# Attention by pairs of heads, and expert tokens of four experts transposed together

## The reference

```python
def block_attention(q, k, v):        # 8 query heads of 64, 2 key heads; blocks of 128 queries
    s = jnp.einsum('bqkgd,bskd->bkgqs', qblk, k) * scale
    p = jax.nn.softmax(s, axis=-1)
    return jnp.einsum('bkgqs,bskd->bqkgd', p, v)

def expert_choice_ffn(h, router_w, w_gu, w_down):   # 16 experts, each picks cap = 2 * n / 16 tokens
    aff = jax.nn.softmax(xf @ router_w, axis=-1)
    gate, idx = lax.top_k(aff.T, cap)
    xin = xf[idx]
    a, u = jnp.split(jnp.einsum('ecd,edf->ecf', xin, w_gu), 2, axis=-1)
    out = jnp.einsum('ecf,efd->ecd', jax.nn.silu(a) * u, w_down) * gate[..., None]
    return jnp.zeros_like(xf).at[idx.reshape(-1)].add(out.reshape(-1, D))
```

## Time and profile before

| | before |
|---|---|
| median of the runs | 4650.71 us (4649.28 to 4650.81, 3 runs) |
| profiled execution | 4647.39 us |
| its span, first to last instruction | 4645.6 us |
| granted TensorE clock, mean | 0.945 of 2.4 GHz |
| attention stage | 427 us, once |
| experts stage | 914 and 912 us |

### The profile page before, as it was taken

How to read it: one execution, slowest core, us unless ns; L and a number is a source line. 1 busy time by engine, 2 the same in 40 slices (tenths; PEclk the granted TensorE clock), 3 DMA queues, 4 the chain that set the end, 5 groups by cost and what they waited for, 6 DMA issues and landing times. The chain is left out here.

```text
span 4645.6 us, 59698 instructions
## 1 busy us (share of the span) xinstructions
PE 4148.2 (89%) x23973; PEld 3289.7 (71%) x23973; DVE 1825.1 (39%) x3112; ACT 1245.0 (27%) x2593; POOL 200.7 (4%) x304
## 2 busy tenths in 40 slices
PE   5798999999759999999699999999768299999996
PEld 1454456665339999998588888888644199999995
DVE  4324355552351111111248888888832611111111
ACT  1211135552201111111244454444423011111111
POOL 0000000000000000001000000000000001000000
PEclk8899989999879999999799999999889599999998
DMA  6201100003487888777410101110032478888884
GB/s 224 86 14 58 35 1 1 1 1 118 174 273 244 252 249 248 239 239 239 123 29 26 31 16 31 31 31 17 7 137 95 129 224 252 251 252 251 251 249 160
DMA packets 522238, 614.81 MB, mean 132 GB/s; under 512 B 16460, under 2 KB 466632, under 8 KB 521449
## 3 DMA queue, kind: packets, MB, share of 16 engines
q1 hardware_dynamic: 502216, 543.33, 36.0%
q0 software_dynamic: 16832, 58.73, 5.0%
q10 hardware_dynamic: 3040, 10.68, 0.6%
HBM read 558.86 MB, written 53.84 MB: 132 GB/s over the span
## 5 line engine op out<-in xcount | busy, mean ns | idle before, releaser
L1385 PEld LDWEIGHTS moe_pgu<-moe_xT,mw_w 128*128 128x128 f32 x8192 | 1118.7, 191 | 15.6 <-issue 15.6
L1385 PE MATMUL moe_pgu<-moe_xT,mw_w 128*128 128x160 f32 x8192 | 1126.4, 300 | 3.0 <-ACT moe_xT L1431 3.0
L1461 DVE TENSOR_TENSOR moe_hT<-moe_sg,moe_pgu 128x160 f32<-128x160 f32 x256 | 82.3, 322 | 1028.0 <-PE moe_pgu L1385 944.9
L1398 PE MATMUL moe_pol<-mw_w,moe_hT 128*128 128x256 f32 x2048 | 474.6, 385 | 0.8 <-DVE moe_hT L1461 0.8
L1642 PE MATMUL rec_pz<-step_hnT,rec_w 128*128 128x256 f32 x1920 | 425.1, 380 | 10.8 <-DMA rec_w<-in_r_w_in 8.8
L1398 PEld LDWEIGHTS moe_pol<-mw_w,moe_hT 128*128 128x128 f32 x2048 | 379.0, 190 | 52.8 <-DVE moe_hT L1461 1.3
L1642 PEld LDWEIGHTS rec_pz<-step_hnT,rec_w 128*128 128x128 f32 x1920 | 362.8, 191 | 59.7 <-DMA rec_w<-in_r_w_in 9.1
L1439 ACT ACTIVATE moe_sg<-moe_pgu 128x160 f32<-128x160 f32 x256 | 77.8, 304 | 1124.9 <-PE moe_pgu L1385 1124.9
L1431 ACT ACTIVATE moe_xT<-moe_pxt,step_modcol 128x128 f32<-128x128 f32 (+1 forms) x512 | 172.5, 417 | 534.2 <-PE moe_pxt L1371 534.2
L1646 PE MATMUL rec_pz<-rec_w,step_hnT 128*128 128x256 f32 x1280 | 284.8, 381 | 15.2 <-ACT rec_zg L1717 15.2
L1646 PEld LDWEIGHTS rec_pz<-rec_w,step_hnT 128*128 128x128 f32 x1280 | 241.5, 191 | 49.8 <-ACT rec_zg L1717 18.0
(11 more groups left out here) (316 smaller groups left out, 4648.7 us busy)
## 6 DMA issues: line engine op xcount, KB each, us to landing
mw_w<-in_moe_w_gu SPq DMA_DIRECT2D x256, 1024.0 KB, 10.1
mw_w<-in_moe_w_down SPq DMA_DIRECT2D x128, 1024.0 KB, 10.2
mod_w_ring<-in_mod_w SPq DMA_DIRECT2D x24, 1024.0 KB, 14.4
mw_w<-in_mod_w SPq DMA_DIRECT2D x24, 1024.0 KB, 14.3
rec_w<-in_r_w_in SPq DMA_DIRECT2D x40, 512.0 KB, 3.9
scratch_xm<-op_x ACTq DMA_DIRECT2D x20, 512.0 KB, 2.6
scratch_xn<-op_xn POOLq DMA_DIRECT2D x20, 512.0 KB, 5.1
hin_w<-in_e_w_in SPq DMA_DIRECT2D x12, 512.0 KB, 6.7
```

Source lines behind the costliest of these rows:

```text
L1385: m = nc.tensor.matmul(pgu[2 * (f % 2) + part][:, :], w[:, j, k, (f % 2) * P:(f % 2 + 1) * P], xT[:, k, :], start=(k == 0), stop=(k == KD ...
L1398: m = nc.tensor.matmul(pol[q // 2][:, (q % 2) * SW:(q % 2 + 1) * SW], hT[:, k, 0:CL], w[:, 8 + q, k, :], start=(k == 0), stop=(k == KD - 1))
```

## The change

Attention: the items become 40 pairs of heads, the eight context pairs first, then the 32 latent ones. Scores of both heads are issued chunk by chunk, one head in the upper and one in the lower 64 rows of the array, into two buffers of three banks. The transposes of both heads are cut in groups of four (five groups for a latent pair) through one PSUM bank; ScalarE copies the first three groups, VectorE the fourth and fifth. The value products of the pair before stand in four pieces between the groups, both heads in turn, in two halves of the array's columns. ScalarE does one exponential per head over all columns, after its copies; VectorE takes maxima over 1,024 and 256 columns.

Experts: the loops are written out. Context tokens are gathered for four experts at once (128 rows, by a new index list `idx_four` that the route makes with four small matmuls), transposed as whole 128x128 tiles and put into a ring of eight experts' tokens in `hnT`; latent tokens are gathered and transposed per expert. GpSimd's copies of indices go, and its gathers no longer wait for the scatter to land.

```diff
-    items = [(2 * pr + r, t, 0 if t < CT else CT, CT if t < CT else KT - CT)
-             for pr in range(4) for t in range(NT) for r in range(2)]
+    pairs = [(pr, t, 0, CT) for pr in range(4) for t in range(CT)] + [(pr, t, CT, KT - CT) for pr in range(4) for t in range(CT, NT)]
+    tiles = [[(r, a) for r in range(2) for a in range(nk)] for _, _, _, nk in pairs]
+    groups = [[tl[g:g + 4] for g in range(0, len(tl), 4)] for tl in tiles]
+    by_dve = [g >= 3 for gr in groups for g in range(len(gr))]
-        s_ps = ps("s_ps", [P, 3 * 512])
-        t_ps = [ps(f"t_ps{i}", [P, 512]) for i in range(4)]
+        s_ps = ps("s_ps", [P, 2, 3 * 512])
+        t_ps = ps("t_ps", [P, 512])
...
@@ TensorE @@
+            def scores(i, j):
+                pr, t, k0, nk = pairs[i]
+                k, n = chunks[i][j]
+                for r in range(2):
+                    if i:
+                        pe.wait_ge(exped, 2 * (i - 1) + r + 1)
+                    nc.tensor.matmul(s_ps[:, r, k * P:(k + n) * P], qT[64 * r:64 * r + HD, pr, t * P:(t + 1) * P],
+                                     kT[64 * r:64 * r + HD, pr // 2, (k0 + k) * P:(k0 + k + n) * P],
+                                     start=True, stop=True).then_inc(qk, 1)
+            def transposes(i, g):
+                group = groups[i][g]
+                pe.wait_ge(normed, 2 * i + 1 + max(r for r, _ in group))
+                copied(pe, gfirst[i] + g)
+                for n, (r, a) in enumerate(group):
+                    m = nc.tensor.transpose(t_ps[:, n * P:(n + 1) * P], p[:, i % 2, r, a * P:(a + 1) * P], S["ident"][:, :])
+                m.then_inc(tr, 1)
             for i in range(N):
+                ng = len(groups[i])
+                for g in range(ng):
+                    transposes(i, g)
+                    if g == 0 and i + 1 < N:
+                        for j in range(len(chunks[i + 1])):
+                            scores(i + 1, j)
+                    if i and (g or ng == 1):
+                        nk = pairs[i - 1][3]
+                        cuts = [nk * x // max(1, ng - 1) for x in range(ng)] if ng > 1 else [0, nk]
+                        a0, a1 = cuts[max(0, g - 1)], cuts[max(1, g)]
+                        if a1 > a0:
+                            products(i - 1, a0, a1)
...
@@ VectorE @@
             for i in range(N):
                 if i + 1 < N:
-                    softmax(i + 1)
-                if i >= 1:
+                    maxes(i + 1)
+                copy(i, 3)
+                if i + 1 < N:
+                    normalise(i + 1, 0)
+                copy(i, 4)
+                if i + 1 < N:
+                    normalise(i + 1, 1)
+                if i:
                     output(i - 1)
...
...
@@ experts @@
+        ring = hnT[:, :, :].rearrange("p k (s c) -> p k s c", c=CC)
+        turns = [("c", 0), ("l", 0)]
+        for e in range(1, NE):
+            turns += [("l", e)] + ([("c", e // 4)] if e % 4 == 0 else [])
+        def coming(e):
+            return [t for t in (("l", e + 1), ("c", (e + 1) // 4)) if t in turns and (t[0] == "l" or (e + 1) % 4 == 0)]
+            def transposes(turn, g):
+                src = xl if kind == "l" else xc
+                for j in range(4):
+                    m = nc.tensor.transpose(pxt[:, j * P:(j + 1) * P], src[:, (4 * g + j) * P:(4 * g + j + 1) * P], S["ident"][:, :])
+                m.then_inc(tr, 1)
-            with pe.Fori(0, NE - 1) as e:
-                expert(e, False)
-            expert(NE - 1, True)
+            for e in range(NE):
...
+                moves = [(turn, g) for turn in coming(e) for g in range(2)]
+                if moves:
+                    transposes(*moves[0])
+                pe.wait_ge(multiplied, NF * (e + 1))
                 for q in range(4):
...
+                    if q + 1 < len(moves):
+                        transposes(*moves[q + 1])
...
@@ GpSimd @@
+            for e in range(NE):
+                if e + 1 < NE:
+                    gather_l(e + 1)
+                if e % 4 == 0 and e + 4 < NE:
+                    gather_c(e // 4 + 1)
                 scatter(e)
...
@@ route @@
+            for j in range(4):
+                m = nc.tensor.matmul(pt[32 * j:32 * j + CAP[0], 4 * NE:], topf[:, 0, 0:CAP[0]], S["ident"][0:NE, j:NE:4],
+                                     start=True, stop=True, tile_position=(0, 32 * j))
```

More of the change, by code:

```diff
@@ new lines, in transposes, with products @@
+            def transposes(i, g):
[5 more added lines that the diff above has]
+                m.then_inc(tr, 1)
+            def products(i, a0, a1):
+                pr, t, k0, nk = pairs[i]
+                if a0 == 0:
+                    copied(pe, gfirst[i + 1])
+                    if i:
+                        pe.wait_ge(o_out, i)
+                for a in range(a0, a1):
+                    for r in range(2):
+                        m = nc.tensor.matmul(o_ps[64 * r:64 * r + HD, 0:P], v[:, k0 + a, (pr // 2) * HD:(pr // 2 + 1) * HD],
+                                             pT[:, i % 2, r * nk + a, :], start=(a == 0), stop=(a == nk - 1))
+                if a1 == nk:
+                    m.then_inc(pv, 1)
@@ new lines, in _ @@
+            for j in range(len(chunks[0])):
+                scores(0, j)
+            for i in range(N):
+                ng = len(groups[i])
[10 more added lines that the diff above has]
+                            products(i - 1, a0, a1)
@@ L964, in _ @@
+            products(N - 1, 0, pairs[N - 1][3])
         @block.scalar
@@ L1271, in _ @@
             dve.wait_ge(tr2, 1)
+            nc.vector.tensor_copy(idx_four[:, :], pt[:, 4 * NE:])
             for c in range(2):
@@ L1354, in scatter @@
[L1354 to L1360 removed]
+            gather_c(0)
+            gather_l(0)
+            for e in range(NE):
[3 more added lines that the diff above has]
+                    gather_c(e // 4 + 1)
                 scatter(e)
[L1362 removed]
+            pool.wait_ge(l_added, 16 * NE)
@@ L1376, in expert @@
+            for turn in turns[0:2]:
+                for g in range(2):
+                    transposes(turn, g)
+            for e in range(NE):
+                for f in range(NF):
                     for part in range(2):
@@ L1447, in _, with to_xT @@
-            with act.Fori(0, NE - 1) as e:
-                expert(e, False)
-            expert(NE - 1, True)
+            def to_xT(turn, g):
+                kind, n = turn
+                act.wait_ge(tr, after(kind, n) - 1 + g)
+                for j in range(4):
+                    k = 4 * g + j
+                    src = pxt[:, j * P:(j + 1) * P]
+                    if kind == "l":
+                        c, dst = 1, ring[:, k, n % 8, 0:CL]
+                    else:
+                        c, dst, src = 0, ring[:, k, 4 * (n % 2):4 * (n % 2) + 4, CL:CC], src.rearrange("p (s c) -> p s c", c=CP)
+                    r = nc.scalar.activation(dst, src, ACT.Identity, bias=mc[:, layer, 3, c, k:k + 1], scale=mc[:, layer, 4, c, k:k + 1])
+                r.then_inc(xT_out, 1)
@@ new lines, in _ @@
+            for turn in turns[0:2]:
+                for g in range(2):
+                    to_xT(turn, g)
+            for e in range(NE):
+                for f in range(NF):
+                    if NF * e + f >= 2:
+                        act.wait_ge(multiplied, NF * e + f - 1)
+                    act.wait_ge(gu_mm, 2 * (NF * e + f) + 1)
+                    nc.scalar.activation(sg[:, f % 2, :], pgu[2 * (f % 2)][:, :], ACT.Silu).then_inc(silued, 1)
+                for turn in coming(e):
+                    for g in range(2):
+                        to_xT(turn, g)
```

297 lines of the change are left out of this document (123 added, 174 removed).

## The result

The changed kernel takes 4478.5 us (median of four runs, 4473.4 to 4481.4) against 4650.0 before: a ratio of 0.963, 95% interval 0.9614 to 0.9647. The profiled execution took 4479.9 us (span 4478.1), 167.5 less than that of before, where the forecast had 157.

The account below looks back on a forecast made before the run. The prediction took TensorE, busy 89% of the span, as the bound. Savings of 60.4 us in the experts and 97 in attention, 157 in all, off the 4650.7 us median gave 4494, range 4455 to 4550.

Parts of the forecast that it names:

- The block kept: Experts: a transpose block that stays between down products falls from 0.80 to 0.44 us, saving 0.36.
- the block removed: Experts: a transpose block that goes from between down products saves its whole 0.80 us.
- The first block: Experts: the block covering the wait for the last product of hT saves only 0.23 us.
- cost nothing: Experts: transfers, gathers and ACT's copies take nothing back; 11 us of DMA slack against 2.2 lost per period.
- The end of the stage is the same: Experts: the change neither gains nor loses time at the end of the stage.
- the way back to the full clock: Attention: the first latent pairs, still at half clock, add 1.5 us.
- VectorE's chain: Attention, latent pair: maxima, copy, scaling, copy on VectorE are what is late and give the 8.85 us period.
- A: Attention rival: the row halves take turns, period 10.6 us, 54 us back, 4548; chance 0.07.
- B: Attention rival: neither row nor column halves run together, TensorE binds at 12.3 us a pair, 4602; chance 0.05.
- C: Attention rival: the clock falls to its lower level, 16.1 us a latent pair, 225 back, 4719; chance 0.05.
- D: Experts rival: instruction fetch of the straight code comes late, two layers lose 1,000 us, 5494; chance 0.03.
- E: Experts rival: they turn out bound by transfers and save nothing, 4554; chance 0.02.

Follow-up runs that it names:

- e10: The kernel before with the 32-row context transposes in the experts' blocks replaced by 128-row latent ones, same count: 4598.0 us, ratio 0.9885.
- e6: The changed kernel without the scaling of head 0's probabilities, the reciprocal kept: 4474.9 us.
- e8: The changed kernel with the scaling of head 0's probabilities in two pieces, one before and one behind the last copy of transposes: 4477.0 us, ratio 0.9632.
- e9: The changed kernel with two PSUM banks for transposed blocks instead of one, the scores of both heads sharing five banks: 4449.7 us, ratio 0.9572.
- e7: The changed kernel with all five copies of transposed blocks by ScalarE, none by VectorE: 4567.2 us.
- e3: The kernel before with only the five engines' loops over the experts written out as straight code: 4647.3 us, ratio 0.9998.
- e5: The changed kernel with both heads' value products in the same half of the columns and one more small output copy a pair: 4513.1 us.
- e11: The changed kernel with the 32 latent pairs ahead of the 8 context pairs: 4473.3 us, ratio 0.9619.

## Why the prediction was right

It had 4494 us, 4455 to 4550, with 0.91 for faster; the result is 4478.5. By its steps:

**Experts, 60.4 us forecast, 69.3 found.** The mechanism was right and two terms of the sum were too small. The block kept was priced at 0.36 saved, from 0.80 and 0.44; the block removed at 0.80. Both prices took a block from the last product to the next one and left the product behind it at 3.56 us. Behind equal transposes, or behind another product, it takes 3.45 (e10): so a block kept saves 0.48 and one removed 0.91. The first block was priced too high, 0.23; it saves 0.16 (35.69 to 35.53 us from gate/up to down). An expert with two blocks saves 0.16 + 0.48 + 2 x 0.91 = 2.46, one with four 0.16 + 3 x 0.48 = 1.6, against 2.19 and 1.31; a layer's first expert saves 3.0 (58.75 to 55.75). The transfers gave no wait: the step "cost nothing" held, and the DMA engines stand empty in front of the down loads as before (share 0.00 from 1586 to 1591). The start of the stage was taken as nothing, within 1.5 us a layer; from the route's first product to the first gate/up block it is 1.5 and 0.4 us less, and 1.7 in both layers of the kernel with the experts alone. "The end of the stage is the same" was wrong by 1.5 us a layer.

**Attention, 97 us forecast, 93.6 found.** Start 3.35 (3.5); seven context pairs 31.35 (31.5), at half clock as forecast; the eighth 9.03 (9.5); from the first block of the first latent pair to that of the last one 279.1 (31 x 8.85 and 1.5, 275.9); the last pair 10.4 (9.5). The step that was mis-sized is the way back to the full clock: the first two latent pairs take 11.5 and 10.6 us, 4.4 above the rest, where I had 1.5. The pair that starts at 895 is 0.33 us longer than the others.

The forecast and the median are 15 us apart: experts 9 and ends 3 too little, attention 3 too much, start of the stages 2, and the last 4 because the forecast took a difference of profiled executions (167.5) off a median, where the medians differ by 171.5.

**The pair, 8.85 forecast and found, for half the reason.** The sum followed VectorE's chain, maxima, copy, scaling, copy, and that chain is there with nearly these durations (the copy takes 0.69 us for 0.7, an exponential with the read of its sum 1.41 for 1.45). The 0.09 for two semaphores stood in no row; from block to block behind a copy by ScalarE, where it was a part of 1.34, the trace has 1.36 to 1.39. But the sum put the bank's chain at 4.3 and 5.65 us for blocks 2 and 3 (the trace has 4.30 and 5.66) and didn't follow it past VectorE's two copies. From block to block it is 1.39 us behind a copy by ScalarE and 1.59 behind one by VectorE, so the first block with the scores behind it, 2.91, and the bank's four waits make 2.91 + 1.39 + 1.36 + 1.60 + 1.59 = 8.85. e6 and e8 show that VectorE's chain could be shorter without a gain, e9 that the bank's could not. The "next bound" of 8.5 in my expectations for them was this same omission: 2.91 and four distances of 1.4. That the number came out to the hundredth is luck: had the bank's chain been longer behind block 3, the forecast would not have seen it.

**The rivals.** A (rows in turn): the halves do run together, 2.42 us for both; had they not, the time would have been 4561 and not 4548, beyond the range that was meant to hold it, since the price let 0.4 us a pair vanish in waits and left out the slow return of the clock. B: the columns are worth 1.38 us a pair, the rows 2.14, together 3.5 as priced. C: the clock is 1.00 in the latent pairs from 720 to 970. The Trainium skill, TensorE: Matmul & The Clock Gate, section PE-mode transpose, says that transposes don't count as busy for the clock in the way that products do. A third of TensorE's work in a pair is transposes, and the trace doesn't agree that this lowers the clock. C was nearer than 0.05 sounds: with 2.3 us of waiting a pair (e7) the clock does fall in every second or third pair. D: 50 packets, no stall (e3). E: no wait for weights.

## What to carry to other kernels

Between products on a full array, count changes of shape as well as instructions: a block of four transposes costs 0.91 us with two shapes and 0.44 with one, and the first figure shows only when the product behind the block is measured too. When two chains of a pipelined loop have nearly the same length, shortening one gives nothing: write down the distances between the uses of each buffer as well as the queue of the engine that looks busy, and test by lengthening or doubling the buffer. When a second buffer is paid for with banks of another, as the scores' was with three of the four banks of transposes here, ask what the other's chain becomes with what is left, for that can be the new bound.

## What the runs showed of the hardware

- A change between transposes and value products and back costs 0.30 us (8.09 to 7.49 us for two round trips with the same matmuls); a block of the experts before, with four changes between 128 and 32 rows, costs 0.47 more than one of four equal transposes.
- Two 64-row halves with fp32 scores run side by side: 2.42 us for the twelve matmul records of both heads, 4.56 in the same rows; one head's six took 2.41 before.
- The granted clock in short, latency-bound work is not settled by the work alone. The context pairs ran at 0.50 with TensorE busy 17.5 of 24 us in the changed kernel, at 1.00 with 5.24 of 8 us in e5, and fell from 1.00 to 0.50 among them behind the latent pairs of e11. A wait of 2.3 us lowered it in some pairs of e7 and not in others. What decides it stays open here.
